# Attention scores over halves of 64 queries: 208 columns for 272, and the gate transposed into the key bank

## The reference

```python
# branch A: 16 query heads on 4 key/value heads, head_dim 64, rotary, a sink per head
keys = concat([ka[:, meta 16], previous block of 128, own block of 128])   # per block of 128 queries
m_meta = ones;  m_prev = kj > qi (and block > 0);  m_cur = kj <= qi
s   = q @ keys.T * HEAD_DIM**-0.5, masked with -inf
mx  = max(max(s), sink);  p = exp(s - mx);  den = sum(p) + exp(sink - mx)
att = (p / den) @ vals
y_a = att * silu(z_a)                      # the gate
# branch B: mLSTM with 4 heads of width 256; then merge, output product, norm
```

## Time and profile before

| | us |
|---|---|
| median of three runs | 2944.84 |
| profiled execution | 2941.8 |
| its span (first to last instruction) | 2940.0 |
| PE busy | 2878.2 (98%) |
| DVE busy | 1479.9 (50%) |
| ACT busy | 1047.7 (36%) |
| POOL busy | 1367.9 (47%) |
| PE busy between 253 and 870 us (heads 1 to 3) | 607.6 of 617.0 |

### The profile page before, as it was taken

How to read it: one execution, slowest core, us unless ns; L and a number is a source line. 1 busy time by engine, 2 the same in 40 slices (tenths; PEclk the granted TensorE clock), 3 DMA queues, 4 the chain that set the end, 5 groups by cost and what they waited for, 6 DMA issues and landing times. The chain is left out here.

```text
span 2940.0 us, 48708 instructions
## 1 busy us (share of the span) xinstructions
PE 2878.2 (98%) x16720; PEld 2467.5 (84%) x16720; DVE 1479.9 (50%) x3713; ACT 1047.7 (36%) x2435; POOL 1367.9 (47%) x1430
## 2 busy tenths in 40 slices
PE   6999999999999999999999999999999999999998
PEld 5888998998987888788878887888788888878887
DVE  5765555555543334433353335333555655566587
ACT  5774544544551212211222113121233323333443
POOL 2224423423342555454545554554454445457586
PEclk9999999999999999999999999999999999999999
DMA  7432212212216544554445443643637675485843
GB/s 259 139 117 97 70 56 91 69 57 97 85 57 203 187 161 136 171 189 154 147 149 198 159 151 128 240 137 118 221 134 282 226 255 203 152 336 199 315 172 129
DMA packets 206950, 473.95 MB, mean 161 GB/s; under 512 B 21090, under 2 KB 76407, under 8 KB 202852
## 3 DMA queue, kind: packets, MB, share of 16 engines
q1 hardware_dynamic: 187204, 409.11, 40.5%
q10 hardware_dynamic: 16800, 52.54, 4.9%
q0 software_dynamic: 2720, 9.32, 1.0%
HBM read 316.49 MB, written 156.38 MB: 161 GB/s over the span
## 5 line engine op out<-in xcount | busy, mean ns | idle before, releaser
L316 POOL TENSOR_TENSOR a_all<-h_raw,a_all 128x256 fp32r<-128x256 f32 x548 | 395.4, 753 | 647.0 <-issue 444.1
L326 PE MATMUL bank_first<-w_all,a_all 128*128 128x384 f32 (+1 forms) x1088 | 414.9, 381 | 2.2 <-POOL a_all L316 2.2
L328 PE MATMUL bank_first<-w_all,a_all 128*128 128x384 f32 (+1 forms) x1088 | 394.3, 362 | 0.0
L327 PE MATMUL bank_first<-w_all,a_all 128*128 128x384 f32 (+1 forms) x1088 | 394.0, 362 | 0.0
L580 ACT ACTIVATE ml_qkt<-ml_pt 128x512 f32<-128x512 f32 x68 | 40.7, 598 | 904.7 <-PE ml_pt L886 904.7
L2599 DVE TENSOR_TENSOR a_all<-sums,a_all 128x512 fp32r<-128x512 f32 x163 | 182.4, 1120 | 167.2 <-ACT a_all L2473 166.3
L326 PEld LDWEIGHTS bank_first<-w_all,a_all 128*128 128x128 f32 x1088 | 204.2, 188 | 52.2 <-issue 28.4
L705 DVE TENSOR_TENSOR ml_qk<-bank_first,bias_all 128x512 f32<-128x512 f32 x66 | 45.7, 692 | 370.8 <-ACT ml_kw L584 370.8
L1388 ACT ACTIVATE at_sm<-at_sm,at_nmx 128x272 f32<-128x272 f32 x272 | 138.8, 511 | 235.8 <-DVE at_nmx L1592 235.8
L328 PEld LDWEIGHTS bank_first<-w_all,a_all 128*128 128x128 f32 x1088 | 204.2, 188 | 22.1
L326 PE MATMUL bank_second<-w_all,a_all 128*128 128x512 f32 x544 | 220.1, 405 | 1.8 <-ACT w_all L203 1.1
(11 more groups left out here) (515 smaller groups left out, 7679.3 us busy)
## 6 DMA issues: line engine op xcount, KB each, us to landing
w_split<-w_early SPq DMA_DIRECT2D x140, 512.0 KB, 3.1
h_raw<-h_t SPq DMA_DIRECT2D x121, 512.0 KB, 4.5
w_all<-w_split SPq DMA_DIRECT2D x34, 1024.0 KB, 14.1
stage<-l_chunks_in SPq DMA_DIRECT2D x45, 512.0 KB, 6.6
w_rest<-w_split SPq DMA_DIRECT2D x16, 1024.0 KB, 10.0
w_early<-w_split SPq DMA_DIRECT2D x14, 1024.0 KB, 7.5
w_plain<-l_x_t_in SPq DMA_DIRECT2D x17, 512.0 KB, 4.9
h_t<-h_raw SPq DMA_DIRECT2D x17, 512.0 KB, 5.8
```

The costliest lines, as they stand in the source:

```text
L316: q = nc.gpsimd.tensor_tensor(k.h_lo[:, u, j:j + 2], k.h_raw[:, u, j:j + 2], k.h_hi[:, u, j:j + 2].bitcast(F32), ALU.subtract)
L326: nc.tensor.matmul(out, hi[:, j], k.w_hi[:, j, col:col + n], start=(j == 0), stop=False)
L327: nc.tensor.matmul(out, hi[:, j], k.w_lo[:, j, col:col + n], start=False, stop=False)
L328: last = nc.tensor.matmul(out, lo[:, j], k.w_hi[:, j, col:col + n], start=False, stop=(j == KT - 1))
```

## The change

Queries and keys are taken in halves of 64. For the lower 64 queries of a tile (`e` = 0) the key bank `kt[:, u, 0]` holds the previous block's lower half, the meta keys, the own lower half and the previous block's upper half; for the upper 64 queries (`e` = 1) `kt[:, u, 1]` holds the own upper half, the meta keys, the own lower half and the previous upper half. Both have 64 + 16 + 64 + 64 = 208 columns, and every key outside them is masked for the whole half. So a query head has two score products, into the lower and the upper 64 rows of its bank, each of 64 rows, 64 weight columns and 208 moving columns. The masks no longer alternate, and `omask` and its copies are gone. `next_keys` puts this tile's keys into the other bank for the next tile.

The transposed weights come as 80 rows (first half or upper half, and meta) and 128 rows. The value products are, per pair of query heads, two over `vbc` (128 keys, 128 queries) and four over `va` (80 keys, 64 queries). Meta keys are rows 64 to 79 of `va`, so that `smm`, its transpose, `ptm`, `vm` and the meta products go. POOL writes `vbc` and `va` with four operations per tile where `vs` took one (five in tile 0). The gate is transposed into columns 256 to 511 of `p_t`, the keys' bank, after `next_keys` has read it (`kn_ready`); the wait for `z_ready` goes, and the wait for `gt_ready` moves from block B to the query/key transposes.

```diff
-    NK = NMETA + 2 * P
+    NK = NMETA + 3 * HD
+    META, LOW, LATE = HD, HD + NMETA, 2 * HD + NMETA
-        kt = sb("kt", [P, NK])
-        vs = sb("vs", [P, 2, HD])
-        vm = sb("vm", [P, 2, W])
+        kt = sb("kt", [P, 2, 2, NK])
+        kts = sb("kts", [HD, P])
+        va = sb("va", [P, 2, 2, HD])
+        vbc = sb("vbc", [P, 2, HD])
...
+        def gate_bank():
+            return p_t[:, 2 * P:2 * P + W]
...
             def keep_v(a, t, m, u):
                 pool.wait_ge(qkv_ready, m + 1)
                 if not is_first(m, 1):
                     pool.wait_ge(o_done, m)
...
-                nc.gpsimd.tensor_tensor(vs[:, key_slot(a, u), :], v, k.ones[:, 0:HD], ALU.mult).then_inc(v_ready, 1)
+                G.tensor_tensor(vbc[0:HD, u, :], lower, one[0:HD], ALU.mult)
+                G.tensor_tensor(va[0:HD, 1 - u, 0, :], lower, one[0:HD], ALU.mult).then_inc(v_step, 1)
+                pool.wait_ge(v_step, s0 + 1)
+                G.tensor_tensor(vbc[HD:P, 1 - u, :], upper, one[HD:P], ALU.mult).then_inc(v_step, 1)
+                pool.wait_ge(v_step, s0 + 2)
+                G.tensor_tensor(va[0:HD, u, 1, :], upper, one[HD:P], ALU.mult).then_inc(v_step, 1)
+                pool.wait_ge(v_step, s0 + 3)
...
+                pool.sem_inc(v_ready, 1)
...
-                act.wait_ge(p_tr, (GRP + 1) * (m + 1))
-                nc.scalar.activation(ptm[:, :], p_t[:, META:META + P], ACT.Copy).then_inc(pt_ready, 1)
                 act.wait_ge(gate_tr, m + 1)
-                nc.scalar.activation(gt[:, :], p_b[:, W:2 * W], ACT.Copy, scale=0.5).then_inc(gt_ready, 1)
+                nc.scalar.activation(gt[:, :], gate_bank(), ACT.Copy, scale=0.5).then_inc(gt_ready, 1)
...
-                V.tensor_copy(kt[:, NMETA + ks * P:NMETA + (ks + 1) * P], p_t[:, 2 * P:3 * P]).then_inc(kt_ready, 1)
+                V.tensor_copy(kt[:, u, :, LOW:LATE], k_low.unsqueeze(1).to_broadcast([P, 2, HD]))
+                V.tensor_copy(kt[:, u, 1, 0:HD], k_high).then_inc(kt_ready, 1)
                 if tile0:
                     sample_keys(a)
+                    next_keys(u)
...
-                if tile0:
-                    V.tensor_copy(omask[:, :], amask[:, 1, :]).then_inc(omask_ready, 1)
-                elif ks == 0:
-                    V.tensor_copy(omask[:, NMETA:NMETA + P], amask[:, 3, NMETA:NMETA + P]).then_inc(omask_ready, 1)
                 V.tensor_tensor(esl[:, :], nmx[:, :], sink[:, sk:sk + GRP], ALU.add).then_inc(den_step, 1)
+                if not tile0:
+                    next_keys(u)
...
-                V.tensor_copy(smm[:, :, 0:NMETA], sm[:, :, 0:NMETA]).then_inc(smm_ready, 1)
...
+            def next_keys(u):
+                V.tensor_copy(kt[:, 1 - u, :, LATE:NK], p_t[:, 2 * P + HD:3 * P].unsqueeze(1).to_broadcast([P, 2, HD]))
+                V.tensor_copy(kt[:, 1 - u, 0, 0:HD], p_t[:, 2 * P:2 * P + HD]).then_inc(kn_ready, 1)
...
             def gate_transposed(m):
                 pe.wait_ge(den_step, 4 * m + 4)
+                pe.wait_ge(kn_ready, m + 1)
...
-                    pe.wait_ge(kt_ready, m)
-                    pe.wait_ge(pt_ready, (GRP + 1) * m)
+                    pe.wait_ge(gt_ready, m)
...
                 if more:
-                    if not is_first(m, 1):
-                        pe.wait_ge(gt_ready, m)
                     block_b(an, m + 1, 1 - u, last)
...
-                    T.matmul(p_t[:, META:META + HD], meta_rep[:, :], vs[0:NMETA, key_slot(a, u), :],
-                             start=True, stop=True).then_inc(rep_done, 1)
...
+                    T.transpose(pbank(g)[0:LOW, 0:P], sm[:, g, 0:LOW], k.ident[:, :])
+                    T.transpose(pbank(g)[:, P:2 * P], sm[:, g, LOW:NK], k.ident[:, :]).then_inc(p_tr, 1)
...
+                    for i in range(2):
+                        T.matmul(p_o[i * HD:(i + 1) * HD, j * P:(j + 1) * P], vbc[:, u, :], pt[:, 2 * j + i, P:2 * P],
+                                 start=j == 0, stop=False, skip_group_check=True)
+                    for e in range(2):
                         for i in range(2):
+                            last_o = T.matmul(p_o[i * HD:(i + 1) * HD, j * P + e * HD:j * P + (e + 1) * HD],
+                                              va[0:LOW, u, e, :], pt[0:LOW, 2 * j + i, e * HD:(e + 1) * HD], start=False,
+                                              stop=j == JD - 1, skip_group_check=True)
...
                 for g in groups:
                     r = (g % 2) * HD
-                    T.matmul(pbank(g)[:, 0:NK], qt[r:r + HD, g // 2, :], kt[r:r + HD, :], start=True,
-                             stop=True).then_inc(s_done, 1)
+                    for e in range(2):
+                        q = T.matmul(pbank(g)[e * HD:(e + 1) * HD, 0:NK], qt[r:r + HD, g // 2, e * HD:(e + 1) * HD],
+                                     kt[r:r + HD, u, e, :], start=True, stop=True)
+                    q.then_inc(s_done, 1)
```

More of the change, by code:

```diff
@@ L123, in const_arrays @@
         c["reset"][h * NT, starts] = NEG
[L125 to L130, removed]
+    q, k, upper = r[:, None], np.arange(HD)[None, :], r[:, None] >= HD
+    no, meta = np.zeros((P, HD), bool), np.ones((P, NMETA), bool)
+    mixed = np.where(q < NMETA, np.arange(NMETA)[None, :] <= q, True)
+    own, low, late = HD + k <= q, k <= q, HD + k > q
+    rows = [np.concatenate([no, mixed, no, no], 1), np.concatenate([upper & own, meta, low, no], 1),
+            np.concatenate([np.where(upper, own, k > q), meta, low, late], 1)]
     c["amask"] = np.stack([np.where(m, 0, NEG) for m in rows], 1).astype(f)
-    c["meta_rep"] = (r[None, :] % MROWS == np.arange(NMETA)[:, None]).astype(f)
-    c["meta_own"] = (r[:, None] // MROWS == np.arange(GRP)[None, :]).astype(f)
     rb, rt = r // (GRP * DT), r % DT
@@ L1298, in keep_v @@
                     pool.wait_ge(o_done, m)
-                if isinstance(m, int) and m % NT == 0 and m:
-                    pool.wait_ge(kvo_ready, 4 * a)
-                v = qkv[:, VC:ZC]
-                nc.gpsimd.tensor_tensor(vs[:, key_slot(a, u), :], v, k.ones[:, 0:HD], ALU.mult).then_inc(v_ready, 1)
+                if t in (0, NPT):
+                    if t == 0 and a:
+                        pool.wait_ge(kv_out, 16 * a * (2 * NB + 4))
+                        pool.wait_ge(smp_pe, PE_N * a)
+                    G.tensor_tensor(kvo[:, t // NPT, 1, :], qkv[:, VC:ZC], k.ones[:, 0:HD], ALU.mult).then_inc(kvo_ready, 1)
+                lower, upper, one = qkv[0:HD, VC:ZC], qkv[HD:P, VC:ZC], k.ones[:, 0:HD]
+                s0 = 3 * m + a + (1 if t else 0)
+                G.tensor_tensor(vbc[0:HD, u, :], lower, one[0:HD], ALU.mult)
[5 more added lines that the diff above has]
+                pool.wait_ge(v_step, s0 + 3)
+                if t == 0:
+                    G.tensor_tensor(va[HD:HD + NMETA].rearrange("p a b n -> p (a b) n"),
+                                    qkv[0:NMETA, VC:ZC].unsqueeze(1).to_broadcast([NMETA, 4, HD]),
+                                    one[0:NMETA].unsqueeze(1).to_broadcast([NMETA, 4, HD]), ALU.mult).then_inc(v_step, 1)
+                    pool.wait_ge(v_step, s0 + 4)
+                pool.sem_inc(v_ready, 1)
             keep_v(0, 0, 0, 0)
@@ L1321, in slot @@
                 if not (last and a == KVH - 1):
-                    keep_v(a + 1 if last else a, t, m + 1, 1 - u)
+                    keep_v(a + 1 if last else a, 0 if last else t + 1, m + 1, 1 - u)
             all_steps(KVH, slot)
@@ L1948, in sample_scores @@
                     T.matmul(p_s[i][:, P:2 * P], rows, kc[:, a % 2, NB, :], start=True, stop=True)
-                    T.matmul(p_s[i][:, 2 * P:3 * P], rows, kt[0:HD, NMETA + key_slot(a, m % 2) * P:
-                                                              NMETA + (key_slot(a, m % 2) + 1) * P], start=True, stop=True)
+                    T.matmul(p_s[i][:, 2 * P:3 * P], rows, kts[:, :], start=True, stop=True)
                     for b in range(4):
@@ L1972, in sample_values @@
                     T.matmul(o[:, cols], spt[:, i, P:2 * P], vc[:, a % 2, NB, :], start=True, stop=False, skip_group_check=True)
[L1973 removed]
+                    T.matmul(o[:, cols], spt[:, i, 2 * P:], kvo[:, 0, 1, :], start=False, stop=False,
                              skip_group_check=True)
```

123 lines of the change are left out of this document (43 added, 80 removed).

## The result

The changed kernel takes 2910.7 us (median of 4 runs, 2910.4 to 2913.8). The kernel before, run beside it, takes 2944.1 (4 runs, 2940.5 to 2946.6). The ratio is 0.989 with a 95% interval of 0.987 to 0.990. The forecast was 2909. The profiled execution has a span of 2908.9 us, against 2940.0 before: 31.1 less, where my sum said 35.8.

A forecast was written before the change was run, and what follows sets the result against it. PE, busy 98%, bounds the kernel, with DVE's rotation chain nearly as long; 27.0 + 3.6 + 5.2 = 35.8 us off the profiled 2941.8 leaves 2906.0, with 3.0 for the median 2909; range 2898 to 2936.

The forecast's parts named there:

- Four abreast: PE's scores stage: eight 64x64 products run four at a time, stage 0.86 us for 1.12, 0.26 gained.
- The rotation is what is late next: DVE's rotation then delays block B to 507.73: gain 0.28 us a tile, not 0.60, PE idle some 0.3.
- The period: Time from tile to tile in head 2: near 11.00 us, against 11.54 before.
- rival 1: Scores: only two products run abreast, stage 1.55 us, kernel 2948, within noise; chance 0.07.
- rival 2: Rotation does not start sooner, `qkv` held at 505.30; 15 of the 36 us missing, 2924; chance 0.13.
- rival 3: Scores: products sharing rows cannot overlap, stage 1.90 us, kernel slower at 2972; chance 0.05.
- rival 4: DVE gives nothing back but PE's saving is whole: another 16 us, 2893; chance 0.05 with the like.
- Head 0: DVE's own chain sets the pace in 14 tiles: -0.26 us a tile, 3.6 us, bounds 0 and -0.6 a tile.
- Tile 0: First tile of each of four heads: about 1.3 us gained each, 5.2 in all, ends 0 and 2.5 each.
- Behind attention: Part of the kernel after attention: no change, attention's gain reaches the end undiminished.
- The price I gave for POOL's value copies when uncovered: POOL's four value copies instead of one: expected hidden; uncovered, at most 1.2 us extra.

The follow-up runs named there:

- one_row: Changed kernel with all eight score products on row half 0, so groups 1 and 3 repeat 0 and 2 (for timing only): 2953.5 us.
- whole_m: Changed kernel with one score product of 64x128 weights and 208 columns per group instead of two of 64x64 (for timing only): 2913.7 us.
- fillers: Changed kernel with the two removed small DVE copies put back where they stood, as writes to scratch: 2911.7 us.
- v_late: Changed kernel where POOL's value copies in head 0 also wait for the end of DVE's rotation: 2910.0 us.
- pad2: Changed kernel with two extra 128x128 PE transposes, output not read, behind the value products of 63 tiles: 2913.5 us.
- pad5: Changed kernel with five extra 128x128 PE transposes, output not read, behind the value products of 63 tiles: 2924.0 us.
- bank_pb: Changed kernel with the gate transposes back in block B's bank, behind the wait for z, as before the change: 2913.7 us.

## Why the prediction was right, point by point

**Four abreast: right.** The stage was put at 0.86 and is 0.86; `one_row` and `whole_m` confirm both parts of its formula. The Trainium skill (TensorE: Matmul & The Clock Gate, "Part 3: Packing small matmuls") lets a weight load overlap a running product only where the row group differs. By that the upper and lower query halves could not overlap. The stage of 0.86, `one_row`'s 1.55, and the value products that share all 128 rows, disagree with it. The Trainium skill (TensorEngine Tiling (Array Packing), "Tiling Modes") lists 64x64 as four tiles, and the trace agrees: the stage takes the four steps of 0.173 us that four abreast need.

**The rotation is what is late next: right, with its size.** `qkv` was to follow the transposes by 0.20 and does; block B was to start 2.83 after them (504.90 to 507.73) and starts 2.84 after (489.78 to 492.62). The wait of some 0.3 before L1852 is there, and its slack is 0.25. The period was put at 11.00 and is 11.02. Rivals 1, 2 and 3 are refuted by these rows, rival 4 by the wait itself.

**Head 0: the term was mis-sized, 1.5 for 3.6 us.** Step by step: the masks came as forecast (0.295 apart for 0.36). The first mask starts 0.76 after the stage's start (121.56 to 122.32), 0.25 sooner than before (122.86 to 123.87), where I had 0.16. The copies of the keys cost their 0.33. `smm` and `omask`, 0.17 in my sum, gave nothing (`fillers`). That makes -0.25 - 0.26 + 0.33 = -0.18. POOL's copies beside the rotation cost 0.11 (`v_late`), which I had not in the sum at all: I had asked whether POOL's extra work was covered, not whom it disturbs. A gain of 0.07 is left, and 0.08 is measured.

**Tile 0: 4.0 for 5.2 us**, inside its bounds. Its parts I did not measure singly, and the four differ (0.7, 1.3, 1.1 and 0.8); the first also holds the start of the program.

**Behind attention: +1.4 where I had 0.** The price I gave for POOL's value copies when uncovered (1.2 us) falls due once, at the end of head 3. There POOL's chain is dense: value copies, split of `h`, split of weights, and PE waits for the last. POOL and PE in the changed kernel:

```profile
838.70 0.50 POOL L1294 TENSOR_TENSOR at_kvo<-at_qkv,at_ones 128x64 f32<-128x64 f32 x1
...
840.87 2.80 POOL L311 TENSOR_TENSOR a_all<-h_raw,a_all 128x256 fp32r<-128x256 f32 x4 [0.24 <-POOL at_va L1302]
...
843.80 8.32 POOL L232 TENSOR_TENSOR w_all<-stage,w_all 128x256 fp32r<-128x256 f32 x12
```

```profile
846.79 0.64 PE L321 MATMUL bank_second<-w_all,a_all 128*128 128x512 f32 x1 [3.06 <-issue]
847.23 0.63 PE L322 MATMUL bank_second<-w_all,a_all 128*128 128x512 f32 x1
```

and both in the kernel before:

```profile
874.95 8.33 POOL L237 TENSOR_TENSOR w_all<-stage,w_all 128x256 fp32r<-128x256 f32 x12
```

```profile
877.94 0.47 PE L326 MATMUL bank_second<-w_all,a_all 128*128 128x512 f32 x1 [1.05 <-ACT w_all L203]
```

PE starts 2.99 after the start of POOL's last stretch. Before it was 2.99 too, but PE's wait was 1.05 us: PE arrives earlier now and POOL, with 2.2 us of value work (838.70 to 840.87) for 0.3, later. Counted from the last `sm` transposes (841.37, before 873.86), PE starts 5.4 us after them for 4.1, and `pad2`, `pad5`, `bank_pb` and `fillers` have the same 5.4. That is the 1.3 us of POOL.

It is not the whole of it, though. Behind this wait of 3.06 us the granted clock is at its lower level, 1.2 GHz (0.52 from 846.79 to 850.20): the first eight products stand 0.43 us apart for 0.23. When PE takes up the next stage (`ml_pc`), the changed kernel is 2.7 us behind, 1.4 of it from these products. `pad5` has the same wait of 3.06 and no fall, and is 1.3 less behind. The rest of the program then took 2054.2 us for 2055.5, which gives 1.3 back; why stays open, and the same rest took between 2052.4 and 2056.8 in the other traces. So the 1.4 is a sum of +1.3, +1.4 and -1.3, and that it looks like the price of POOL's copies is chance. No run took POOL's copies away alone.

The forecast of 2909 is within 2 us of the median. It is closer than its sum deserves: 4.7 us were missing in the profiled pair, of which the median gives back about 3, since it had been counted from a median 3.0 above the profiled execution.

## What to carry to other kernels

- When work is taken from the busiest engine, ask first which chain lies next to it and how far behind. Here PE could have given 0.77 us a tile, 0.52 came out, and one moved wait brought 0.20 of the rest back. Padding the engine shows such slack to a few hundredths.
- Before pricing a small instruction by its duration, look whether the next one waits for the result of the one in front of both. There it is free to keep and worthless to remove.
- An engine's idle time is not empty because nothing in it is long. Moving work into it needs a list of what in it has a date, and of what the neighbour engine does then.

## What the runs showed of the hardware

- **Issue order inside a stage** changes 0.02 us of the stage on PE (0.86 and 0.88) and makes the kernel 12.6 us longer, for the most part through the time at which the first group is complete.
- **POOL beside DVE.** A rotation step of 32 columns goes from 0.18 to 0.31 us, a 128-column scaling from 0.29 to 0.85, while POOL runs a value copy (64 x 64) or a part of its split (128 x 256). `v_late` shows the first by moving the copy; the second is read from the overlap in the traces. `esl` (L1590, 4 columns, 497.97 above) takes 0.66 beside the split and 0.16 where POOL is idle. Instructions that read a bank keep their length: the masks (L1583) take 0.37 or 0.38 with POOL running and without. The Trainium skill (GPSIMD Engine Reference, "Specifications", the row on SBUF interfaces) says that the two engines share their SBUF interfaces, with contention where DVE reads two inputs from SBUF or runs in a two-port mode; the rows agree that they collide. `esl` and L1482 read two inputs and no bank. L1481 does so too and keeps its 0.32, but it was under way (117.26) when POOL's copy began (117.31), and there the copy took 0.44, where in `v_late` it took 0.31. The one that starts later seems to wait; no run tests that.
- **The clock after a tile 0 is a matter of the execution.** The changed kernel and `v_late` do the same in tile 0 of head 2, with the same waits of PE in it (0.63 and 1.44 us). The granted clock (the column after POOL's busy time) stayed at its upper level, 2.4 GHz, in one and fell to the lower, 1.2 GHz, in the second of these waits in the other. First the changed kernel, then `v_late`:

```profile
467.00:470.00 3.00, 2.58 (x43) 2.23 (x39) 2.89 (x10) 1.49 (x5) 0.26 (x1) 1.00 0.00 0
```

```profile
467.00:470.00 3.00, 3.00 (x26) 2.54 (x23) 2.88 (x10) 1.47 (x4) 0.00 (x0) 0.50 0.00 0
```

The next tile took 13.1 us in `v_late` and 11.6 in the changed kernel. In heads 1 and 3 it was 1.1 and 1.2 longer, and the last tile of attention 1.5: 5.4 us in all, which hides the 1.3 of head 0 in this execution (2915.2 us, the longest of the four). The other three left no trace. This is why the tile medians were the better measure.
